# Hybrid attention and state-space layer on one core: weights laid out by unit, tanh for two gates, fifteen weight units split on GpSimd

## The reference, cut to what matters

```python
h = rms_norm(x, g_norm)                       # x: 512 tokens x 2048
proj = h @ w_in                               # q, k, v, att_gate, q_idx, k_idx, w_idx, u, ssm_gate, merge
q, k, q_idx, k_idx = (partial_rotary(t) for t in ...)
# for each block of 128 queries:
logits = einsum("bqhd,bsd->bqhs", q_idx, k_idx) * 64 ** -0.5      # 16 index heads
score = einsum("bqhs,bqh->bqs", relu(logits), w_idx)              # keys of later chunks: -inf
_, sel = top_k(score, 128)
att = softmax(q @ k[sel].T * 128 ** -0.5) @ v[sel]                # 8 heads, 2 key heads
y_a = (att * silu(att_gate)) @ w_att_out
s = gelu(s5_ssm(u, ...)); s = s * sigmoid(s @ w_glu + b_glu)
y_b = (s * silu(ssm_gate)) @ w_ssm_out
gates = sigmoid(merge + b_merge)
out = rms_norm(x + (gates0 * y_a + gates1 * y_b) @ w_out, g_final)
```

## Time and profile before

| what | us |
|---|---|
| three runs: median (lowest to highest) | 1156.45 (1155.94 to 1157.69) |
| the profiled execution, its own time | 1155.37 |
| its span, first to last instruction | 1153.6 |
| PE busy | 1123.0 (97%) |
| DVE busy | 757.3 (66%) |
| ACT busy | 446.1 (39%) |
| POOL busy | 40.8 (4%) |

### The profile page before, as it was taken

How to read it: one execution, slowest core, us unless ns; L and a number is a source line. 1 busy time by engine, 2 the same in 40 slices (tenths; PEclk the granted TensorE clock), 3 DMA queues, 4 the chain that set the end, 5 groups by cost and what they waited for, 6 DMA issues and landing times.

```text
span 1153.6 us, 13392 instructions
## 1 busy us (share of the span) xinstructions
PE 1123.0 (97%) x5318; PEld 927.0 (80%) x5318; DVE 757.3 (66%) x1266; ACT 446.1 (39%) x594; POOL 40.8 (4%) x47
## 2 busy tenths in 40 slices
PE   5999999999999999999999999999999999999997
PEld 3998888887787788888777777888888888788885
DVE  6698579899655566527877888344234545777585
ACT  5732333333364452223233323343322222654374
POOL 1000000001100000000000000000000000000000
PEclk9999999999999999999999999999999999999999
DMA  9745344457443127565545666444657432577655
GB/s 326 214 117 146 110 119 137 110 121 156 124 115 87 55 73 176 132 140 145 149 120 149 148 135 147 125 147 146 146 137 155 110 96 60 192 254 266 233 189 207
DMA packets 189854, 170.53 MB, mean 148 GB/s; under 512 B 13408, under 2 KB 163168, under 8 KB 188768
## 3 DMA queue, kind: packets, MB, share of 16 engines
q1 hardware_dynamic: 168032, 133.84, 38.9%
q0 software_dynamic: 12800, 33.56, 13.4%
q10 hardware_dynamic: 8960, 2.29, 0.9%
HBM read 163.37 MB, written 37.75 MB: 174 GB/s over the span
## 4 chain that ended last, share of the span: by engine, by line
PE 85%; DVE 10%; DMA 2%; ACT 1%; issue 1%; ACTq 0%; DVEq 0%
PE banks L558 22%; PE banks L560 21%; PE banks L559 21%; PE banks L801 4%; PE banks L803 4%; PE banks L802 4%; DVE w_lo L1281 2%; DMA w_raw<-in_w_in 2%; PE banks L708 2%; DVE score L1418 2%; PE banks L689 1%; DVE small L1417 1%; PE banks L758 1%; PE banks L698 1%; PE banks L774 1%
## 5 line engine op out<-in xcount | busy, mean ns | idle before, releaser
L558 PE MATMUL banks<-act_hi,w_hi 128*128 128x512 f32 (+1 forms) x1088 | 422.7, 388 | 4.2 <-DVE w_lo L1281 4.2
L560 PE MATMUL banks<-act_hi,w_lo 128*128 128x512 f32 (+1 forms) x1088 | 417.3, 384 | 0.0
L559 PE MATMUL banks<-act_lo,w_hi 128*128 128x512 f32 (+1 forms) x1088 | 417.1, 383 | 0.0
L558 PEld LDWEIGHTS banks<-act_hi,w_hi 128*128 128x128 f32 x1088 | 204.7, 188 | 44.8 <-DVE w_lo L1281 5.9
L560 PEld LDWEIGHTS banks<-act_hi,w_lo 128*128 128x128 f32 x1088 | 204.5, 188 | 38.4
L1281 DVE TENSOR_TENSOR w_lo<-w_raw,w_hi 128x2048 fp32r<-128x2048 f32 x80 | 183.2, 2290 | 79.4 <-ACT w_hi L903 78.5
L559 PEld LDWEIGHTS banks<-act_lo,w_hi 128*128 128x128 f32 x1088 | 204.8, 188 | 35.1 <-issue 0.2
L903 ACT ACTIVATE w_hi<-w_raw 128x2048 fp32r<-128x2048 f32 (+1 forms) x81 | 154.1, 1903 | 110.5 <-DMA w_raw<-in_w_in 110.2
L1759 DVE TENSOR_TENSOR w_lo<-w_raw,w_hi 128x512 fp32r<-128x512 f32 (+1 forms) x64 | 67.5, 1086 | 34.5 <-ACT w_hi L1185 34.5
L1185 ACT ACTIVATE w_hi<-w_raw 128x512 fp32r<-128x512 f32 (+1 forms) x64 | 59.6, 949 | 60.8 <-DMA w_raw<-w_sums 37.2
L1168 ACT ACTIVATE gate<-gate,g_cols 128x512 f32<-128x512 f32 x16 | 11.6, 724 | 128.5 <-DVE gate L1721 128.5
(11 more groups left out here) (299 smaller groups left out, 1466.1 us busy)
## 6 DMA issues: line engine op xcount, KB each, us to landing
w_raw<-in_w_in SPq DMA_DIRECT2D x67, 1024.0 KB, 5.5
w_sums<-in_w_out POOLq DMA_DIRECT2D x24, 1024.0 KB, 8.5
w_raw<-w_sums SPq DMA_DIRECT2D x32, 512.0 KB, 4.0
w_sums<-w_sums POOLq DMA_DIRECT2D x8, 1024.0 KB, 11.0
w_raw<-in_w_att_out SPq DMA_DIRECT2D x8, 1024.0 KB, 5.5
w_raw<-in_w_out SPq DMA_DIRECT2D x16, 512.0 KB, 4.9
x_tok<-in_x SPq DMA_DIRECT2D x4, 1024.0 KB, 8.0
w_raw<-in_w_ssm_out SPq DMA_DIRECT2D x4, 1024.0 KB, 5.1
```

Of the source, the lines that this page charges most:

```text
L558: nc.tensor.matmul(out_ap, wh, x_hi[k], start=(j == 0), stop=False)
L559: nc.tensor.matmul(out_ap, wh, x_lo[k], start=False, stop=False)
L560: last = nc.tensor.matmul(out_ap, wl, x_hi[k], start=False, stop=(j == n - 1))
```

## The change

The input weights are laid out by the host in the order in which the units are loaded, each tile 128 rows of 8 KB in one piece; before, a unit is 128 x 16 pieces of 512 bytes. The key unit is laid out in the same way. Six of the seven small DMAs move from ACT's queue to POOL's, behind POOL's split of the key unit, and three of them have a semaphore of their own. Fifteen units (`POOL_UNITS`) are split by POOL and not by DVE: 4 to 8, and 23 to 32. The tokens for the norm are loaded before unit 2 and before unit 3, not behind them. The copied index queries have four buffers (two in `q_raw`, two in `ang`), `index_keys` stands after head pair 3 and not after 4, and the norm's row is turned earlier in unit 3. The gates 6 and 7 go through Tanh with one more DVE instruction of 128 x 512 each, in place of Silu.

```diff
+W_BLOCKS = ((COL_QI, 8), (COL_K, 2), (COL_V, 2), (COL_Q, 8), (COL_AG, 8), (COL_U, 4), (COL_SG, 4), (COL_MERGE, 32))
+POOL_UNITS = (4, 5, 6, 7, 8, 23, 24, 25, 26, 27, 28, 29, 30, 31, 32)
+            "w_tiles": np.stack([w_in[:, :, col:col + P] for col in cols]),
...
+        def q_slot(i):
+            return (q_raw if i % 4 < 2 else ang)[:, i % 2, 0:SEQ - P]
             def w_in_cols(col):
-                return w_in_v[:, :, col:col + P]
+                return w_tiles[W_TILE[col]]
@@ SP, index query units
-                load(u, KD, w_in_cols(COL_QI + P * i))
                 if i == 1:
                     load_tokens(0)
                     load_tokens(1)
                 if i == 2:
                     load_tokens(2)
                     load_tokens(3)
+                load(u, KD, w_in_cols(COL_QI + P * i))
@@ POOL
+            def low_on_pool(u):
+                pool.wait_ge(high_done, u)
+                pool.tensor_tensor(w_lo[:, u % SLOTS, :], w_raw[:, u % SLOTS, :], w_hi[:, u % SLOTS, :].bitcast(F32), ALU.subtract
+                                   ).then_inc(pool_split, 1)
...
+            for u in POOL_UNITS:
+                if u < UNIT0["attgate"]:
+                    low_on_pool(u)
+            def gates_through(last):
+                for u in range(behind[0], min(last, max(POOL_UNITS) - 2) + 1):
+                    i = u - UNIT0["attgate"]
+                    if i < 6:
+                        pool.wait_ge(row_ready, 1)
+                        pool.wait_ge(tile_free, TILE0["attgate"] + i + 1)
+                        pool.tensor_tensor(gate_a[:, i, :], gate_a[:, i, :], row[:, :], ALU.mult).then_inc(a_gate_scaled, 1)
+                    if u + 2 in POOL_UNITS:
+                        low_on_pool(u + 2)
@@ PE
-            for i in range(1, 8):
-                qi(1 + i, i, (lambda k: turn_row() if k == 5 else None) if i == 2 else None)
+                qi(1 + i, i, (lambda k: turn_row() if k == 2 else None) if i == 2 else None)
@@ ACT
-            act.wait_ge(params_loaded, 4 * 16)
+            act.wait_ge(params_loaded, 16)
...
             for i in range(2, 8):
-                act.wait_ge(qidx_ready, i - 1)
+                if i >= 4:
+                    act.wait_ge(qidx_ready, i - 3)
                 query_tile(i)
...
-                nc.scalar.activation(gate_a[:, i, :], gate_a[:, i, :], ACT.Silu).then_inc(a_gate_ready, 1)
+                    nc.scalar.activation(ang[:, i - 6, :], gate_a[:, i, :], ACT.Tanh).then_inc(a_gate_ready, 1)
@@ DVE
                 for u in range(lows[0], min(u_last + 1, LAST_UNIT)):
+                    if u in POOL_UNITS:
+                        continue
...
-                if i == 4:
+                if i == 3:
                     index_keys()
...
+                        if h >= 6:
+                            link(v.scalar_tensor_tensor(gate_a[:, h, :], ang[:, h - 6, :], 1.0, gate_a[:, h, :], ALU.add, ALU.mult))
```

More of the change, by code:

```diff
@@ L41 @@
     int(c) for c in np.cumsum((0,) + WIDTHS[:-1]))
+W_BLOCKS = ((COL_QI, 8), (COL_K, 2), (COL_V, 2), (COL_Q, 8), (COL_AG, 8), (COL_U, 4), (COL_SG, 4), (COL_MERGE, 32))
+W_TILE = {col + P * i: n for n, (col, i) in enumerate((c, i) for c, m in W_BLOCKS for i in range(m))}
 HALF = D // 2
@@ L139, in laid_out, with hybrid_kernel @@
     params = [columns(a) for a in (given["a_re"], given["a_im"], steps, given["g_norm"], given["b_merge"], given["b_glu"], direct)]
[L140 removed]
+    w_in = given["w_in"][0].reshape(KD, P, -1).transpose(1, 0, 2)
+    cols = [col + P * i for col, n in W_BLOCKS for i in range(n)]
+    return {"w_key": np.ascontiguousarray(w_in[:, :, COL_KI:COL_KI + IDX_DIM + IDX_HEADS]),
+            "w_tiles": np.stack([w_in[:, :, col:col + P] for col in cols]),
+            "x_fm": np.ascontiguousarray(given["x"][0].T.reshape(KD, P, SEQ).transpose(1, 0, 2)),
             "params": np.ascontiguousarray(np.concatenate(params, axis=1))}
[L144 to L146 removed]
+def hybrid_kernel(nc, x, positions, b_re, b_im, c_re, c_im, w_glu, w_att_out, w_ssm_out, w_out, g_final,
+                  w_key, w_tiles, x_fm_in, params, c_cols, c_ident, c_parity, out):
     w_att_v = w_att_out[0].rearrange("(k p) n -> p k n", p=P)
@@ L518, in _ @@
                                ).then_inc(early_split, 1)
[L521 to L530, removed]
+            pool.dma_start(pos_i[:, :], positions.to_broadcast([P, SEQ])).then_inc(consts_loaded, 16)
+            pool.dma_start(cols[:, :], c_cols).then_inc(consts_loaded, 16)
+            pool.dma_start(ident[:, :], c_ident).then_inc(ident_loaded, 16)
+            pool.dma_start(par[:, 0:3, :].rearrange("p a j -> p (a j)"), params[:, 0:48]).then_inc(late_params_loaded, 16)
+            pool.dma_start(g_cols[:, 0:36], params[:, 64:100]).then_inc(late_params_loaded, 16)
+            pool.dma_start(small[:, D_COL:D_COL + TILES], params[:, 100:108]).then_inc(late_params_loaded, 16)
+            for u in POOL_UNITS:
+                if u < UNIT0["attgate"]:
+                    low_on_pool(u)
+            behind = [UNIT0["attgate"]]
+            def gates_through(last):
[7 more added lines that the diff above has]
+                        low_on_pool(u + 2)
+                behind[0] = max(behind[0], last + 1)
             step = 0
@@ L571, in wait_split @@
                 else:
-                    pe.wait_ge(split_done, u - 1)
+                    if u in POOL_UNITS:
+                        pe.wait_ge(pool_split, POOL_UNITS.index(u) + 1)
+                    else:
+                        pe.wait_ge(split_done, u - 1 - sum(p < u for p in POOL_UNITS))
             h_hi = [act_hi[:, k, :] for k in range(KD)]
@@ L933, in _ @@
                 nc.scalar.activation(w_hi[:, 1, here], w_raw[:, 1, here], ACT.Copy).then_inc(first_high, 1)
-            act.wait_ge(tile_done, 1)
-            nc.scalar.activation(k_raw[0:IDX_DIM, :], stream_bank[0][0:IDX_DIM, :], ACT.Copy).then_inc(kidx_raw, 1)
-            nc.scalar.activation(w_idxT[IDX_DIM:IDX_DIM + IDX_HEADS, :], stream_bank[0][IDX_DIM:IDX_DIM + IDX_HEADS, :],
-                                 ACT.Copy).then_inc(tile_free, 1)
             def squares_of(t):
@@ L945, in query_tile @@
             def query_tile(i):
-                copy_tile(1 + i, q_raw[:, i % 2, 0:SEQ - P], stream_bank[(1 + i) % 2][:, 0:SEQ - P])
+                copy_tile(1 + i, q_slot(i), stream_bank[(1 + i) % 2][:, 0:SEQ - P])
+            squares_of(0)
+            act.wait_ge(tile_done, 1)
+            nc.scalar.activation(k_raw[0:IDX_DIM, :], stream_bank[0][0:IDX_DIM, :], ACT.Copy).then_inc(kidx_raw, 1)
+            nc.scalar.activation(w_idxT[IDX_DIM:IDX_DIM + IDX_HEADS, :], stream_bank[0][IDX_DIM:IDX_DIM + IDX_HEADS, :],
+                                 ACT.Copy).then_inc(tile_free, 1)
             high_through(2)
-            squares_of(0)
             squares_of(1)
+            squares_of(2)
             query_tile(0)
-            high_through(3)
-            squares_of(2)
             squares_of(3)
             nc.scalar.activation(small[:, 8:12], small[:, 0:4], ACT.Sqrt, bias=small[:, 236:237], scale=1.0 / D).then_inc(root_ready, 1)
-            query_tile(1)
             high_through(4)
@@ L1024, in silu_of @@
                     act.wait_ge(a_gate_scaled, i + 1)
+                    nc.scalar.activation(gate_a[:, i, :], gate_a[:, i, :], ACT.Silu).then_inc(a_gate_ready, 1)
                 else:
                     act.wait_ge(tile_free, TILE0["attgate"] + i + 1)
-                nc.scalar.activation(gate_a[:, i, :], gate_a[:, i, :], ACT.Silu).then_inc(a_gate_ready, 1)
+                    nc.scalar.activation(ang[:, i - 6, :], gate_a[:, i, :], ACT.Tanh).then_inc(a_gate_ready, 1)
             for i in range(HEADS):
```

30 lines of the change are left out of this document (15 added, 15 removed).

## The result

| kernel | runs | median us (lowest to highest) | ratio to before, 95% interval |
|---|---|---|---|
| before, same chip | 6 | 1155.88 (1154.41 to 1157.69) | |
| after | 6 | 1161.55 (1160.72 to 1162.32) | 1.005 (1.0038 to 1.0063) |

The changed kernel is slower by 5.7 us. Its profiled execution took 1161.35 us with a span of 1159.6; before these were 1155.37 and 1153.6.

A forecast was written before the change was run, and what follows sets the result against it. PE was taken to bound the kernel almost everywhere. Index queries with the start +1.0, selection -4.8 and softmax +8 gave +4.2 us on 1155.4, so 1159.6, or 1160.5 as median; range 1150.5 to 1167.

The forecast's parts named there:

- POOL's split: One 128x2048 split on POOL takes 4.53 us and holds DVE's two-input SBUF and double-rate operations meanwhile; DVE needs 2.29.
- masking and gating run on: In the softmax, DVE's masking and gating, reading PSUM and one SBUF tensor, were assumed not to stand beside POOL.
- The start: Up to PE's first product: key lands at 6.3 to 7.2 us, product at 7.6 to 8.5 not 11.8; gain 4.
- The index queries: Units 1 to 8: POOL's splits stop DVE, the start's lead is lost, and the fifth index item comes 1.0 us later.
- The selection: Splits 23 to 26 go to POOL, DVE's maxima do not stand, all four PE waits go: -4.8 us.
- The softmax: Units 28 to 32: POOL's splits hold DVE's scaling and PE waits for the probabilities: +8 us, ends 3.5 and 12.
- The sum: Whole kernel: +1.0 - 4.8 + 8 = +4.2 us on the profiled execution, 1159.6; median 1160.5.
- the kept lead: Rival for the index queries: DVE's losses fall into time it waited anyway; -2.6 us in all, 1153.9; chance 20%.
- the cheap softmax: Rival for the softmax: DVE's scaling slips in ahead of POOL, costing 3.5; -0.3 us in all, 1156.2; chance 17%.
- it goes further: Rival: each long halt drops the clock, index queries cost 3, softmax 12; +10.2 us in all, 1166.6; chance 13%.

The follow-up runs named there:

- halves: The changed kernel with each of the fifteen POOL splits cut into two instructions of 1024 columns; 1156.43 us, 1.0008 of before.
- pieces: The changed kernel with each of the fifteen POOL splits cut into four instructions of 512 columns; 1149.5 us, 0.995 of before.
- full_keyfirst: The changed kernel, all fifteen units on POOL, with the key's load issued ahead of the first two pieces of x; 1161.34 us, 1.0053 of before.
- late: The changed kernel with units 4 to 8 back on DVE, POOL splitting only 23 to 32; 1155.05 us, 0.9999 of before.
- five: The changed kernel with only units 23 to 27 split by POOL; 1145.38 us, 0.9915 of before.
- none: The changed kernel with no unit split by POOL, all else kept; 1148.74 us, 0.9938 of before.
- silu: Against five: Silu back in place of Tanh for gates 6 and 7, without the extra DVE operation; 1147.51 us, 0.993 of before.
- order9: Against the changed kernel with POOL on 4 to 8 and 23 to 27 only: `index_keys` moved behind unit 9's split; 1153.15 us, 0.9976 of before.

## Why the prediction was right, and where not

Forecast 1160.5 us, measured 1161.55, slower as forecast. Step by step:

- POOL's split: 4.53 forecast, 4.61 the median. That it holds DVE's two-input and double-rate operations was right, and so was the assumption that masking and gating run on. Shown by the trace after, and by halves and pieces. The trace agrees with the rule of the Trainium skill ("SBUF — State Buffer", section "Who interferes with whom") named in the prediction: two inputs in SBUF stood (4.32 us), the double-rate scaling stood (4.49), masking and gating did not (0.56, 0.28).
- The start: 4 us of gain forecast, 1.97 measured. This is the step that failed. I put the key's landing at 6.3 to 7.2 us from the rate of a busy stretch, as if only the key and the first x (1.15 MB) had to move. It came at 8.5, and by then 2.35 MB had moved: the key shared the queue with loads issued behind it, and from 0 to 9 us the rate was 281 GB/s, not 422. It was no accident of one trace: in the nine kernels with this order of the loads the first product came at 9.0 to 10.5, in the four with the key first at 8.1 to 8.8. So the order of issue decided it.
- The index queries: fifth item +1.0 forecast, +3.18 measured. Unit 9's split was forecast for 96.2, PE started on it at 98.33; the fifth item for 112.6, it came at 114.49. Both are some 2.0 late, which looks like the missing 2.0 of the start, and full_keyfirst, where start and fifth item moved together, supports that in its trace. But on the way two errors cancel. POOL's split of unit 5 was forecast to end at 53.0 and ended at 56.66, 3.7 late. The start explains 2.0 of it, if what follows moves with it as in full_keyfirst (first product and this split both 1.1 earlier). The rest is that I had tokens and weights landing sooner still, and they did not. From there to the fifth item I had 59.6 us and it took 57.8, above all because the next three rotations stood for 11.8 us together, not 13.2. The mechanism, that DVE's chain is slower with POOL's help than without, is shown by late and by five.
- The selection: -4.8 forecast, -5.4 measured; the waits went. But I credited all of it to POOL, and none shows 3.4 for POOL's splits; the other 2.0 came with the rest of the change. That the term came out near is partly luck.
- The softmax: +8 forecast, +8.3 measured. The waits came at all five units. Forecast with what PE needs to start again: 0.6, 2.2, 3.4, 1.0, 2.8; measured as waits alone: 0.39, 1.91, 3.17, 0.54, 2.48. But the size of the sum is partly luck. I let 3.7 us of the old halt at gate 7 stand and charged unit 30 only 1.8 more. That halt went with the table loads: where POOL splits none of these units, the stage takes 98.5 us, 2.2 less than before, and silu puts the tanh at 2.6 there, where I had given it 1.3 at most. Against that POOL's splits cost 10.6, and the part that I had not counted is a second stretch at half clock.
- The sum: +4.2 forecast, +6.0 in span. The term mis-sized is the first one, start and index queries together: +3.2 and not +1.0.
- The rivals: the kept lead is ruled out by the fifth item at 114.49, the cheap softmax by five waits. Of "it goes further" half came: the index stage at its bad end (+3.2), and a second stretch at half clock, but the softmax stayed at +8.3, not +12.

## What to carry to other kernels

What a helper engine costs is not its own time but what the helped one cannot do meanwhile. Here five splits on POOL beside the softmax cost 10.6 us and spared DVE 11 us of work that PE was not waiting for, while beside the selection, whose maxima do not stand, five splits gained 3.4. Ask what runs next to the moved work, not how busy the helper is, and if operations that stand must run beside it, cut the helper's instruction short. Then look twice at each halt of PE: behind some of them (of 1.8 to 4.1 us in these traces) a stretch at half clock cost 1.7 us more, behind others it did not come.

## What was not expected of the hardware

The drop of the granted clock behind a halt is not certain. In after the halt of 3.21 us for unit 9 brought none (1.00 behind it), halts of 3.17 and 2.48 brought 3.4 us each at 0.50; in order9 one of 4.1 did. In full_keyfirst a halt of 3.2 us for the same unit 9 brought 3.4 us at 0.53, in pieces one of 2.8 brought 3.4 at 0.51. The executions of one kernel differ in this too: full_keyfirst went from 1158.4 us at a mean granted clock of 0.995 to 1165.2 at 0.991, late from 1153.0 at 0.997 to 1157.3 at 0.992, while five, at 0.996 to 0.998, scatters by only 1.2 us. That goes with such stretches as the cause of the scatter; only one execution of each kernel was profiled, so it is not shown.

The layout took the DMA packets from 189,854 to 56,879 for the same 170.53 MB, and the median landing of a 1 MB unit from 5.5 to 4.9 us. PE waited for no such load before, and nothing in the traces turns this into time.
